# The first half of a chain of device-memory sums, placed one stage earlier on GpSimd's queue

## What is computed

```python
def _mlstm_branch(x, ...):          # layer 1
    ...
    return (hb * silu(z)) @ w_out   # 1024 x 2048 times 2048 x 1024

def _pool_branch(x, w_in, w_group, scale, w_out):   # layer 2
    proj = x @ w_in
    u, z = proj[..., :2048], proj[..., 2048:]
    ...                              # trailing means of u, per group
    mixed = einsum("bsgc,gcd->bsgd", pooled, w_group) * scale
    return (mixed * silu(z)) @ w_out

for i in range(2):
    x = layer_norm(alpha * x + branch_i(x), post_ln_g[i], post_ln_b[i])
```

## Time and profile before

| | |
|---|---|
| median of 3 runs | 1404.59 us (1404.48 to 1404.92) |
| profiled execution | 1404.74 us, its span 1403.0 us |
| PE busy | 1388.0 us, 99% of the span |
| DVE, ACT, POOL busy | 1119.1, 727.1, 152.4 us |
| DMA queues | SP's queue 38.4% of 16 engines' span, GpSimd's 12.2% |
| TensorE clock granted | 0.998 |

### The profile page before, as it was taken

One profiled execution on the slowest core, in us unless ns is written; L12 is line 12 of the kernel. 1 busy time (PEld: TensorE's weight loads), 2 busy tenths in 40 slices (PEclk: granted clock), 3 DMA queues, 4 the chain that ended last, 5 costly groups with the idle time before them and its releaser, 6 DMA issues.

```text
span 1403.0 us, 18567 instructions
## 1 busy us (share of the span) xinstructions
PE 1388.0 (99%) x6488; PEld 1155.2 (82%) x6488; DVE 1119.1 (80%) x1739; ACT 727.1 (52%) x1202; POOL 152.4 (11%) x251
## 2 busy tenths in 40 slices
PE   9999999999999999999999999999999999999997
PEld 7788888888888888888878888878888888888886
DVE  7988879798887978878674455797888888889976
ACT  6865646556564655656543345664333343336341
POOL 2002011110100111010000001001111111100021
PEclk9999999999999999999999999999999999999999
DMA  5024425353342534336487666444665555689661
GB/s 229 33 69 124 110 69 150 91 140 93 106 128 54 165 82 137 105 99 195 136 292 254 211 207 217 131 128 105 166 162 153 140 161 153 170 271 358 217 198 75
DMA packets 103435, 213.26 MB, mean 152 GB/s; under 512 B 10912, under 2 KB 27552, under 8 KB 102192
## 3 DMA queue, kind: packets, MB, share of 16 engines
q1 hardware_dynamic: 90544, 178.53, 38.4%
q0 software_dynamic: 12800, 33.56, 12.2%
HBM read 170.04 MB, written 75.56 MB: 175 GB/s over the span
## 4 chain that ended last, share of the span: by engine, by line
PE 62%; DVE 2%; DMA 1%; issue 0%; POOL 0%; ACT 0%; SPq 0%; DVEq 0%; POOLq 0%; ACTq 0%
PE wide L2774 13%; PE wide L2775 12%; PE wide L2776 12%; PE ps_state L2774 2%; PE ps_state L2775 2%; PE ps_state L2776 2%; PE ps_inter L2774 2%; PE ps_inter L2775 2%; PE ps_inter L2776 2%; PE ps_s L2774 1%; PE ps_intra L2774 1%; PE ps_s L2775 1%; PE ps_intra L2775 1%; PE ps_s L2776 1%; PE ps_intra L2776 1%; PE ps_intra L2946 1%
## 5 line engine op out<-in xcount | busy, mean ns | idle before, releaser
L2775 PE MATMUL wide<-xa,inb 128*128 128x512 f32 x576 | 224.5, 390 | 0.0
L2774 PE MATMUL wide<-xb,inb 128*128 128x512 f32 x472 | 189.3, 401 | 0.1
L2776 PE MATMUL wide<-xb,inb 128*128 128x512 f32 x472 | 184.3, 391 | 0.0
L2775 PEld LDWEIGHTS wide<-xa,inb 128*128 128x128 f32 x576 | 108.4, 188 | 19.7
L2775 PE MATMUL wide<-xa,blk 128*128 128x512 f32 x320 | 124.5, 389 | 0.0
L2776 PEld LDWEIGHTS wide<-xb,inb 128*128 128x128 f32 x472 | 88.6, 188 | 18.9
L2774 PEld LDWEIGHTS wide<-xb,inb 128*128 128x128 f32 x472 | 88.8, 188 | 18.0 <-DVE inb L1870 1.2
L2774 PE MATMUL wide<-xb,blk 128*128 128x512 f32 x256 | 99.7, 389 | 0.8 <-ACT zz L1741 0.8
L2776 PE MATMUL wide<-xb,blk 128*128 128x512 f32 x256 | 99.6, 389 | 0.0
L1789 ACT ACTIVATE wy<-wy_raw 128x1024 fp32r<-128x1024 f32 x56 | 59.4, 1062 | 61.9 <-DMA wy_raw<-y_block 61.6
L2774 PE MATMUL wide<-xa,inb 128*128 128x512 f32 x208 | 83.1, 400 | 2.8 <-DVE inb L1870 1.8
(11 more groups left out here) (431 smaller groups left out, 3802.6 us busy)
## 6 DMA issues: line engine op xcount, KB each, us to landing
in_raw<-in_w_in SPq DMA_DIRECT2D x45, 512.0 KB, 4.3
wy_raw<-y_block SPq DMA_DIRECT2D x56, 256.0 KB, 4.4
mw_raw<-h_block SPq DMA_DIRECT2D x53, 256.0 KB, 3.4
m_sum<-in_w_out POOLq DMA_DIRECT2D x48, 256.0 KB, 4.6
h_block<-f_buf SPq DMA_DIRECT2D x48, 256.0 KB, 3.2
w_sum<-in_pool_w_out POOLq DMA_DIRECT2D x48, 256.0 KB, 4.3
a_raw<-in_pool_w_z SPq DMA_DIRECT2D x16, 512.0 KB, 4.0
a_raw<-folded SPq DMA_DIRECT2D x16, 512.0 KB, 4.4
```

Source lines behind the costliest of these rows:

```text
L2774: pe.matmul(dst, a[0], b[0], start=first, stop=False, skip_group_check=more)
L2775: pe.matmul(dst, a[0], b[1], start=False, stop=False, skip_group_check=more)
L2776: return pe.matmul(dst, a[1], b[0], start=False, stop=last, skip_group_check=more)
```

## The change

GpSimd issues the first 32 of the pool layer's 64 sum steps before the `deviation`s of layer 1, each behind a tick of layer 1's output projection: step n waits for `k_done >= n + 1`. The other 32 stay where they were, with the same waits. No transfer, no buffer and no arithmetic is added or taken away.

```diff
+W_EARLY = W_STEPS // 2
...
+            for n in range(W_EARLY):
+                pool.wait_ge(k_done, n + 1)
+                sum_step(n, p_out, w_sums, w_summed)
+
             for t in range(NC):
                 deviation(t, 0)
...
-            for n in range(W_STEPS):
+            for n in range(W_EARLY, W_STEPS):
                 pool.wait_ge(prod, 4 + n + n // 4)
                 sum_step(n, p_out, w_sums, w_summed)
```

## The result

The changed kernel takes 1429.51 us (median of 4 runs, 1423.76 to 1431.04) against 1404.53 us before (4 runs, 1404.1 to 1404.92). The ratio is 1.017, 95% interval 1.0141 to 1.02: slower by 25 us, where 10.5 had been forecast and the range ended at 1422. The profiled execution has a span of 1428.8 us, 25.8 more than the one before.

A forecast was written before the change was run, and what follows sets the result against it. PE, busy 1388.0 of 1403.0 us, was taken to bound the kernel. 1404.7 plus 2.5 at K8 plus 8 for the stall before K43, minus 0 gain, gave 1415.2, stated as 1415 us; range 1404 to 1422.

The forecast's parts named there:

- case C: Rival: at 6 us a step, step 31 goes at 885 or later, 22 us at K43, over 1424 in all; chance 0.04.
- the 875 of the forecast: Issue time in us taken for step 31 on GpSimd, against a limit of 867, giving a stall of 8 us before K43.
- the gain side: Steps leaving the time after 948 us give back at most 1 us of PE's idleness; taken as 0.
- First term, K8: Early steps delay the residual's load, so PE starts tick K8 later: 2.5 us, bounds 1 and 4.4.
- the upper end: At K8, SP's loads pay each early step's full share of the DMA engines: 4.4 us.
- Second term, the latest issue of step 31: Step 31 must be issued by 867.0 us, or the deviations behind it on GpSimd delay DVE and PE's K43.
- Second term, the pace: Early steps' interval on GpSimd, slowed by SP's share, puts step 31 at 875: a stall of 8 us before K43.
- The slope: Step interval grows 2.1 us per whole of SP's DMA share, extrapolated from two later windows; puts step 31 at 878.
- The bounds of 4.84: Unloaded pace of 4.84 us a step everywhere would issue step 31 at 853, under 867, costing nothing.
- A: Rival: only K8 pays, steps average below 5.3 us, deviations find GpSimd free; 1405.7 to 1409 us, chance 0.20.
- B: Rival: not slower, residual at K8 undelayed and pace holds; 1403.7 to 1405.5 us, chance 0.14.
- The form of B: Ticks, not landings, set the early steps' pace: step 31 at 836.5, needing a step under 4.3 us.

The follow-up runs named there:

- e4: Changed kernel with 16 early steps instead of 32, step n waiting for n + 9 ticks, so the first goes after K9: 1407.33 us, ratio 1.0011.
- e8: e2 with SP loading the residual of tiles 2 and 3 ahead of the second group's 1 MB of weights: 1406.76 us, ratio 1.0012.
- e5: Changed kernel with each of its 32 early steps moving 64 of 128 rows, 128 KB instead of 256: 1406.16 us, ratio 1.0011.
- e9: The changed kernel again, unchanged, on one chip beside two other runs: 1423.55 us (4 runs, 1419.11 to 1428.15), ratio 1.0119.
- e7: Changed kernel with 30 early steps instead of 32: 1413.2 us (5 runs, 1409.25 to 1416.42), ratio 1.0052.
- e2: Changed kernel with all 32 early steps, but the four urgent deviations placed between steps 25 and 26: 1409.61 us, ratio 1.003.
- e1: Changed kernel with 24 early steps instead of 32, the other 40 in the pool layer's input projection: 1410.59 us, ratio 1.0029.

## Why the prediction was wrong

Both waits came at the places that the prediction named. Their size was that of case C, by its own bound (step 31 at 885 or later, over 1424 in all), which had a chance of 0.04. The number was wrong because of one term, the pace of the chain. Since K43 follows step 31 one for one, the waits at K8 and F16 don't add to the loss of the changed kernel; they only shorten the stall. What adds up is this: step 31 came 13.0 us later than the 875 of the forecast, K43 followed it after 5.03 us where I had 4.5 (0.5), and its tick ran at the lower clock (1.9). Together that is 15.4 us, and 25.8 exceeds the forecast 10.5 by 15.3. With step 31 at 875 and all else as measured, the profiled execution would have taken 1430.7 - 13.0 = 1417.7 us, within the range.

*What bounds the kernel, and the gain side.* Right. 960 to 1350 stays without a new wait, step 63 went at 1232.5 (1206 plus the shift of 26), and nothing came back.

*First term, K8.* Right in place and size: 1.9 us for a forecast 2.5, between the bounds of 1 and 4.4. e4 and e8 take it away by keeping the steps or the megabyte from the residual's load, e5 halves it. The view of the DMA queues for 710 to 730 us of the changed kernel shows the displacement:

```profile
q1 hardware_dynamic: 3161, 6.37, 85.7%
q0 software_dynamic: 362, 0.77, 19.0%
```

SP's queue moved 6.37 MB where it had moved 342 GB/s * 20 us = 6.8, and lost 9 points of share to GpSimd's 19. The rule of going round packet by packet, from "DMA: Bandwidth & Descriptors" (Queues, rings and completion order) of the Trainium skill, stood for the upper end; the measured wait is nearer to the lower.

*Second term, the latest issue of step 31.* Nearly right. I had 4.5 us from its issue to K43 (1.9 to the root, 2.6 through DVE); three traces have 5.03.

*Second term, the pace: the step that failed.* "The slope gives 878", and then 875 was taken: 5.56 us a step. Step 31 went at 887.98 in the changed kernel, 5.97 a step, and at 885.91 in e9, 5.87. By parts of the chain, mean interval in us (e7 has the same instructions up to step 29; the forecast is that of the slope, without the 3 us taken off):

| steps | forecast | changed | e9 | e7 |
|---|---|---|---|---|
| 0 to 4 | 5.7 | 6.3 | 6.4 | 6.0 |
| 4 to 8 | 6.2 | 6.9 | 6.6 | 6.7 |
| 8 to 27 | 5.6 | 5.8 | 5.6 | 5.3 |
| 27 to 31 | 5.5 | 5.5 | 5.9 | |

Up to step 8, in the fullest stretch, all three are slower than the slope said, by 3 to 5.5 us in all. Behind it the slope is right for e9, too low for the changed kernel and too high for e7. The view of the DMA queues for 757 to 866 us, first of the changed kernel, then of e7, shows that SP's share isn't what tells the two apart:

```profile
q1 hardware_dynamic: 15952, 21.29, 61.6%
q0 software_dynamic: 1904, 4.98, 23.0%
...
w_sum<-in_pool_w_out POOLq DMA_DIRECT2D x14, 256.0 KB, 6.0
...
q1 hardware_dynamic: 15875, 21.24, 61.6%
...
w_sum<-in_pool_w_out POOLq DMA_DIRECT2D x16, 256.0 KB, 5.1
```

The same bytes of SP at the same share, and the transfers land in 6.0 us in one execution and 5.1 in the other, where the earlier trace rows had 4.3 (each figure is a median over copies and adds together; the prediction read it as that of the adds alone, which is 4.6).

The slope itself stood on less than I thought. One of the seven intervals from 1214.59 to 1251.25, the longest, ended on a wait that the trace puts down to PE, not to a landing:

```profile
1234.40 0.51 POOL L1046 DMA_DIRECT2D w_sum<-w_sum  x1 [6.03 <-PE ps_state L2776]
```

Without its 6.85 us the other six have a mean of 4.97, and the slope is 0.7 us per whole share instead of 2.1, which would give 5.05 us at a share of 0.63. Every execution with full steps was slower than that. So I had a slope from two windows, read partly from a wait of another kind, used it at up to three times the share, and then shaved 3 us off in the direction of the rows that stood farther away. 13 us late in the chain became 12 of stall (20.3 for 8).

*What the prediction lacked.* F16: in the kernel before, DVE had the third group's first operand ready at 811.4 us and PE started F16 at 811.58, so that load had 0.2 us to spare. With steps beside it PE waits 1.9 us; this cost shows in the versions without a stall at K43. And the clock: 1.9 us behind the long stall, in some executions 1.2 to 2.5 more behind each short wait.

*The range.* The pace is multiplied by 31. e7 and the changed kernel differ by 14 us at step 29, and the changed kernel's eight runs go from 1419 to 1431. I had held case C, 6 us a step, "1424 in all" and more, at 0.04. The median of the first four runs and four of all eight lie in it. Both profiled executions (1430.67 and 1428.15) are among the slower ones: the median of all eight is 1426.0, which by the one-for-one rule puts step 31 at about 883, an estimate. The bounds of 4.84 and the slope were treated as ends, though nothing in the trace bounded the pace from above.

*The rivals.* A and B fell with step 31 at 888. The form of B by the 2.6 us of "DMA: Bandwidth & Descriptors" (Anatomy of one DMA) of the Trainium skill fell too: even 128 KB took 4.81 us a step.

*Still open.* Why the same chain takes 5.60 us a step up to step 29 in one execution and 6.10 in another, and so how much of the 13 us is a pace that was sized too low and how much is the execution. It wasn't tied to anything that these views show, and no run here was made for it.

## What to carry to other kernels

A chain of dependent transfers at the head of an in-order queue is a timer: its length times the pace must end before the first small, urgent operation behind it, with a margin for a pace that differed by 9% between two executions here. Put the urgent operations between the steps (e2: 14 to 20 us for a few lines), or don't move the chain at all when nobody waits for its end. When a transfer is added to a full stretch, look for the loads that already arrive last (K8, F16), since they pay at once.

## What the runs showed of the hardware

- A wait of PE of only 2 to 3 us was in some executions followed by a lower granted clock: 0.83 over the 10 us around it, and twelve matmuls in 4.4 to 4.6 us (e1 after 2.75 and 2.36 us, e4 after 1.92). In others it wasn't: e2 waited 3.08 us and the twelve took 2.99.
- Halving a DRAM-to-DRAM step from 256 to 128 KB, beside a queue of SP with a share of 0.6 to 0.9, shortened it only from 5.97 to 4.81 us.
- Moving such steps into a fuller stretch also made the kernel's time less steady: 1419 to 1431 us over eight runs of the changed kernel, where 15 runs of the kernel before on one of these chips go from 1404.3 to 1409.1.
